# The inverse of a chunked RWKV-7 scan: each level's first product for two heads as one 128-row matmul against zero-padded operands

## The reference, cut to what matters

```python
def step(S, inp):
    r_t, w_t, k_t, v_t, a_t, b_t = inp
    sa = jnp.einsum('bhvk,bhk->bhv', S, a_t)
    S = S * w_t[:, :, None, :] + sa[..., None] * b_t[:, :, None, :] + v_t[..., None] * k_t[:, :, None, :]
    y = jnp.einsum('bhvk,bhk->bhv', S, r_t)
    return S, y
```

## Time and profile before

| | |
|---|---|
| median of three runs | 3730.86 us (3730.16 to 3739.53) |
| span of the profiled execution | 3730.1 us |
| TensorE busy, of the span | 93% |
| VectorE, ScalarE, GpSimd busy | 68%, 40%, 32% |
| the scan: its first matmul of the inverse to its last | 1610.2 to 1941.5 us |
| joint steps in it | 73 |

### The profile page before, as it was taken

One profiled execution on the slowest core, in us unless ns is written; L12 is line 12 of the kernel. 1 busy time (PEld: TensorE's weight loads), 2 busy tenths in 40 slices (PEclk: granted clock), 3 DMA queues, 4 the chain that ended last, 5 costly groups with the idle time before them and its releaser, 6 DMA issues. The chain is left out here.

```text
span 3730.1 us, 55202 instructions
## 1 busy us (share of the span) xinstructions
PE 3484.1 (93%) x23684; PEld 2843.4 (76%) x23684; DVE 2548.5 (68%) x2261; ACT 1510.4 (40%) x1620; POOL 1188.1 (32%) x544
## 2 busy tenths in 40 slices
PE   8999999999999998977788999999998999997996
PEld 6778788887877776667776788887877888886875
DVE  5563767678767875966657667678867888857532
ACT  4563533334443336844446432334454122125322
POOL 1225445445532211243433444555531000000211
PEclk9999999999999999978999999999999999998998
DMA  2112123354312243842323133344312222234422
GB/s 101 39 52 65 55 95 110 102 180 140 115 55 99 79 144 111 261 145 83 105 65 125 48 102 107 103 169 151 106 60 95 84 79 74 79 124 100 146 94 107
DMA packets 218755, 387.50 MB, mean 104 GB/s; under 512 B 16321, under 2 KB 118849, under 8 KB 214529
## 3 DMA queue, kind: packets, MB, share of 16 engines
q1 hardware_dynamic: 180944, 311.62, 26.1%
q10 hardware_dynamic: 37568, 72.36, 5.2%
HBM read 277.50 MB, written 105.91 MB: 103 GB/s over the span
## 5 line engine op out<-in xcount | busy, mean ns | idle before, releaser
L3912 POOL MEMSET ssm_toep<- 128x4096 f32 x1 | 3.5, 3512 | 538.9 <-POOLq L3578 538.9
L3439 DVE SCALAR_TENSOR_TENSOR H<-hy_cu,par,H 128x1024 f32<-128x1024 f32 x120 | 153.5, 1279 | 0.0
L270 POOL TENSOR_TENSOR wlo1C<-fast_raw,whi1C 128x1024 fp32r<-128x1024 f32 (+1 forms) x40 | 112.5, 2813 | 112.7 <-ACT whi1C L260 112.7
L270 POOL TENSOR_TENSOR wlo0B<-fast_raw,whi0B 128x1024 fp32r<-128x1024 f32 (+1 forms) x40 | 113.0, 2825 | 106.0 <-ACT whi0B L260 106.0
L270 POOL TENSOR_TENSOR wlo1A<-fast_raw,whi1A 128x1024 fp32r<-128x1024 f32 (+1 forms) x40 | 111.5, 2787 | 104.0 <-ACT whi1A L260 104.0
L270 POOL TENSOR_TENSOR wlo0A<-fast_raw,whi0A 128x1024 fp32r<-128x1024 f32 (+1 forms) x40 | 110.7, 2768 | 103.5 <-ACT whi0A L260 103.5
L270 POOL TENSOR_TENSOR wlo1B<-fast_raw,whi1B 128x1024 fp32r<-128x1024 f32 (+1 forms) x39 | 107.7, 2762 | 112.1 <-ACT whi1B L260 111.9
L3439 DVE SCALAR_TENSOR_TENSOR hy_odd<-hy_cu,par,hy_odd 128x1024 f32<-128x1024 f32 x112 | 143.3, 1279 | 0.0
L1008 DVE TENSOR_TENSOR fast_xl<-fast_xr,fast_xh 128x2048 fp32r<-128x2048 f32 (+1 forms) x42 | 127.7, 3062 | 21.4 <-ACT fast_xh L849 21.4
L270 POOL TENSOR_TENSOR wlo0C<-fast_raw,whi0C 128x1024 fp32r<-128x1024 f32 (+1 forms) x39 | 108.0, 2768 | 104.1 <-ACT whi0C L260 104.0
L2717 PE MATMUL psA<-sc_XX,sc_NT 64*64 64x32 f32 x2560 | 104.8, 232 | 31.8 <-issue 18.8
(11 more groups left out here) (1459 smaller groups left out, 11601.9 us busy)
## 6 DMA issues: line engine op xcount, KB each, us to landing
fast_raw<-ffn_in_dram SPq DMA_DIRECT2D x88, 512.0 KB, 3.9
fast_xr<-ffn_x SPq DMA_DIRECT2D x28, 1024.0 KB, 6.2
fast_raw<-ffn_out_dram SPq DMA_DIRECT2D x32, 512.0 KB, 3.8
sc_ops<-rw_arbkv SPq DMA_DIRECT2D x14, 1024.0 KB, 6.0
wraw1A<-hybrid_in_dram SPq DMA_DIRECT2D x24, 512.0 KB, 3.5
wraw1B<-hybrid_in_dram SPq DMA_DIRECT2D x24, 512.0 KB, 3.5
ffn_x<-fast_g ACTq DMA_DIRECT2D x22, 512.0 KB, 3.2
ffn_x<-fast_e ACTq DMA_DIRECT2D x22, 512.0 KB, 2.8
```

Source lines behind the costliest of these rows:

```text
L270: eng.tensor_tensor(self.slot(wlo, n), self.raw[n], self.slot(whi, n).bitcast(fp32), ALU.subtract)\
L3439: op = dve.scalar_tensor_tensor(out=acc, in0=c[:, j:j + T], scalar=w, in1=acc, op0=ALU.mult, op1=ALU.add)
L3912: pl.memset(toep[:, :, :], 0.0).then_inc(*tick("st_zero"))
```

## The change

The first product of a tile becomes one matmul for both heads. Its stationary operand is NT of the tile with all 128 rows. Its moving operand is 128 rows x (2 heads x 32 columns) out of a new tensor `XT`, where each head's transposed X stands in the rows of one half and zeros stand in the other half, so that the heads don't mix. The result has 64 partitions, those of `half(m % 2)`, and the heads side by side in the columns. ScalarE brings it to the layout of `Wt` with four copies (two by tile parity and two by head) in place of one. The transposes of VectorE write to `XT`, a ring of three chunks, and wait for the first product of three chunks before; VectorE clears `XT` once at the scan's start. NT's ring goes from six to five, and tensors move in SBUF.

```diff
-                self.XX = at("sc_XX", [P, 4, 2, DT, CHUNK], fp32, 114.5)
-                self.NT = at("sc_NT", [P, 6, DT, CHUNK], fp32, 130.5)
+                self.XX = at("sc_XX", [P, 4, DT, CHUNK], fp32, 113.25)
+                self.XT = at("sc_XT", [P, 3, 2, DT, CHUNK], fp32, 121.25)
+                self.NT = at("sc_NT", [P, 5, DT, CHUNK], fp32, 133.25)
...
-            NTS = 6
+            NTS = 5
+            TURNS = 3
...
+            paired = [b.rearrange("p (e g t) -> p e g t", e=2, g=4) for b in bank]
...
+            def part_of_two(t, l):
+
+                return t.rearrange("p e (g b c) -> p e g b c", b=2, c=2 << l)[:, :, :, 0, :]
...
-                            pe.wait_ge(*after("sc_W", ix + 1))
+                            pe.wait_ge(*after("sc_W", 4 * ix + 4))
...
                         for m in range(DT):
                             if w is not None:
-                                for e in range(2):
-                                    mw = pe.matmul(part_of_tile(eight[iw % 2][half(e), m, :], lw, 0), NT[half(1 - e), iw % NTS, m, :],
-                                                   part_of_tile(XX[half(1 - e), cw % 4, 1, m, :], lw, 0), start=True, stop=True)
+                                mw = pe.matmul(part_of_two(paired[iw % 2][half(m % 2), :, m // 2, :], lw), NT[:, iw % NTS, m, :],
+                                               part_of_two(XT[:, cw % TURNS, :, m, :], lw), start=True, stop=True)
                                 if m == DT - 1:
                                     mw.then_inc(*tick("pe_W"))
...
-                        act.activation(part(Wt[l][:, :, :], l, 0), part(eight[i % 2], l, 0), ACT.Copy).then_inc(*tick("sc_W"))
+                        for q in range(2):
+                            for e in range(2):
+                                act.activation(part_of_two(Wt[l][half(e), q:DT:2, :], l), part_of_two(paired[i % 2][half(q), e, :, :], l),
+                                               ACT.Copy).then_inc(*tick("sc_W"))
...
-                            dve.transpose(XX[half(1 - e), n % 4, 1, :, :].rearrange("p m t -> p (m t)"),
-                                          XX[half(e), n % 4, 0, :, :].rearrange("p m t -> p (m t)")).then_inc(*tick(name))
+                            dve.transpose(XT[half(1 - e), n % TURNS, e, :, :].rearrange("p m t -> p (m t)"),
+                                          XX[half(e), n % 4, :, :].rearrange("p m t -> p (m t)")).then_inc(*tick(name))
...
                     def turned(n):
                         dve.wait_ge(*after("sc_eye_added", n + 1))
+                        if n >= TURNS:
+                            dve.wait_ge(*after("pe_W", order[n - TURNS, LEVELS - 1] + 1))
                         turn_over(n, "sc_turned")
...
                     dve.memset(S[:, 0, :, :], 0.0).then_inc(*tick("sc_S"))
+                    dve.memset(XT[:, :, :, :, :], 0.0).then_inc(*tick("sc_clear"))
+                    dve.wait_ge(*after("sc_clear", 1))
```

More of the change, by code:

```diff
@@ L1441, in __init__ @@
                 self.mask = at("sc_mask", [P, 2, CHUNK], fp32, 96)
[L1442 to L1445, removed]
-                self.XX = at("sc_XX", [P, 4, 2, DT, CHUNK], fp32, 114.5)
-                self.NT = at("sc_NT", [P, 6, DT, CHUNK], fp32, 130.5)
+                self.level = at("sc_level", [P, 5, CHUNK], fp32, 184.75)
+                self.first = at("sc_first", [P, CHUNK], fp32, 96.5)
+                self.eye = at("sc_eye", [P, CHUNK], fp32, 97)
+                self.UV = at("sc_UV", [P, 4, 2, DT, HEAD], fp32, 97.25)
+                self.XX = at("sc_XX", [P, 4, DT, CHUNK], fp32, 113.25)
+                self.XT = at("sc_XT", [P, 3, 2, DT, CHUNK], fp32, 121.25)
+                self.NT = at("sc_NT", [P, 5, DT, CHUNK], fp32, 133.25)
                 self.Wt = [at(f"sc_Wt{l}", [P, DT, CHUNK], fp32, k) for l, k in enumerate((144.25, 146.25, 150.25, 68, 70))]
@@ L2531, in rwkv_scan @@
             RING = 4
-            NTS = 6
+            NTS = 5
+            TURNS = 3
             smask, slevel, sfirst, seye, ops, rt, at = room.mask, room.level, room.first, room.eye, room.ops, room.rt, room.at
-            G, BK, UV, XX, Gx, NT, Wt, Z, S, grown = room.G, room.BK, room.UV, room.XX, room.Gx, room.NT, room.Wt, room.Z, room.S, room.grown
+            G, BK, UV, XX, XT, Gx, NT, Wt, Z, S, grown = (room.G, room.BK, room.UV, room.XX, room.XT, room.Gx, room.NT, room.Wt, room.Z,
+                                                           room.S, room.grown)
             bank = [ps[b // 2][:, b % 2, :] for b in range(8)]
@@ L2723, in inverse @@
                                     mx = pe.matmul(part_of_tile(eight[2 + ix % 2][half(e), m, :], lx, 1), Wt[lx][half(e), m, :],
-                                                   part_of_tile(XX[half(e), cx % 4, 0, m, :], lx, 1), start=True, stop=True)
+                                                   part_of_tile(XX[half(e), cx % 4, m, :], lx, 1), start=True, stop=True)
                                 if m == DT - 1:
@@ L2749, in u_step @@
                             for e in range(2):
-                                mm = pe.matmul(eight[place(("U", n))][half(1 - e), m, :], XX[half(e), n % 4, 0, m, :], Z[half(e), n % 2, m, :],
+                                mm = pe.matmul(eight[place(("U", n))][half(1 - e), m, :], XX[half(e), n % 4, m, :], Z[half(e), n % 2, m, :],
                                                start=True, stop=True)
@@ L2824, in to_xx @@
                         for e in range(2):
-                            act.activation(XX[half(e), n % 4, 0, :, :], G[half(1 - e), n % 4, e, :, 0:CHUNK], ACT.Copy).then_inc(*tick("sc_raw"))
+                            act.activation(XX[half(e), n % 4, :, :], G[half(1 - e), n % 4, e, :, 0:CHUNK], ACT.Copy).then_inc(*tick("sc_raw"))
                     def to_gx(n):
@@ L2902, in begin @@
                     def begin(n):
-                        x = XX[:, n % 4, 0, :, :]
+                        x = XX[:, n % 4, :, :]
                         pl.wait_ge(*after("sc_raw", 4 * n + 2))
@@ L2964, in x_out @@
                             dve.wait_ge(*after("sc_XX", order[n, l - 1] + 1))
-                        mine = part(XX[:, n % 4, 0, :, :], l, 1)
+                        mine = part(XX[:, n % 4, :, :], l, 1)
                         dve.tensor_tensor(mine, part(eight[2 + k % 2], l, 1), mine, ALU.add).then_inc(*tick("sc_XX"))
@@ L3006, in rwkv_scan @@
             passed({f"ring_{b}": sum(incs[b::RING]) for b in range(RING)})
-            passed({n: len(order) for n in ("pe_W", "pe_XX", "sc_W", "sc_NT", "sc_XX")})
+            passed({n: len(order) for n in ("pe_W", "pe_XX", "sc_NT", "sc_XX")})
+            passed({"sc_W": 4 * len(order), "sc_clear": 1})
             passed({n: NC for n in ("sc_first", "sc_eye_added", "pe_Z", "pe_U", "pe_ys", "pe_y", "sc_S")})
```

## The result

| | before | after |
|---|---|---|
| median of four runs each | 3734.8 us | 3960.1 us |
| after to before | | 1.0604 (95%: 1.0582 to 1.0625) |
| span of the profiled execution | 3730.1 us | 3954.5 us |
| inverse, first matmul to last | 331.5 us | 550.2 us |
| granted clock over that stretch | 0.89 | 0.76 |

The kernel is 6.0% slower. Of the 224.4 us by which the spans differ, 218.7 lie in the stretch of the inverse.

The account below looks back on a forecast made before the run. TensorE, the scan's busiest engine, was taken as the bound. 3730 + 281 (pauses with mixed clock) + 2 (ScalarE's copies) + 1 (VectorE's clearing) = 4014 us, range 3850 to 4130.

Parts of the forecast that it names:

- The pause at each change of pattern: Joint steps on TensorE: two pauses a tile, 0.15 us each at full level; a step 3.9 us instead of 0.92.
- TensorE's work becomes the period: Scan: other engines are ready long before, so a period is TensorE's work, 28.5 us at full level, 46 at the lower.
- The share of the lower clock: Scan: two thirds of the time at the lower level, nearer to its first 38 us (78%); +281 us with the pauses.
- the prediction's own formula: Scan period with mixed clock: 28.5 / (1 - 0.67 x (1 - 28.5/46)) = 38.2 us.
- The period before: Scan of the kernel before: a period taken as 18.96 us, so the new one is 19.2 us more, x 14.6.
- ScalarE's copies: Scan: four copies for one, 0.29 us each; up to +9 us in joint steps left to the range, +2 counted altogether.
- Clearing, rings, layout: Scan: VectorE's one clearing counted at +1 us, at most 3; `turned`'s new wait and NT's ring of five at nothing.
- the array's quarters bind: Rival, joint steps: no pause within a step, six records a quarter instead of four; 3733 to 3767 us, chance 0.04.
- the number of records does: Rival, joint steps: 48 records instead of 64 take 0.69 us a step, so faster, 3711 us; chance 0.02.

Follow-up runs that it names:

- group_of_eight: Against the kernel after: a joint step issues its eight wide first products, then its sixteen second products, two pattern changes instead of sixteen; 3716.9 us, ratio 0.9953.
- tall_second: Against the kernel after: second products also take all 128 rows, so no pattern change inside a step, order tile by tile kept; 3718.5 us, ratio 0.9956.
- full_columns: Against the kernel after: the wide first product moves all 128 columns instead of 64, sixteen pauses a step stay; 3956.5 us, ratio 1.0597.

## Why the prediction was right

It gave 4014 us in a range of 3850 to 4130, slower at 0.95; measured are 3960 us.

- **The pause at each change of pattern** held to the hundredth: 0.49 us a tile forecast and measured at the full level, 0.75 and 0.76 at the lower. That two blocks' borders tell what happens sixteen times inside a step was the leap, and group_of_eight and tall_second show it right from two sides. The rule of the Trainium skill, "TensorEngine Tiling (Array Packing)", section Tiling Modes, that changing the mode drains TensorE, agrees with them; it gives no price, and the price here is 0.15 us at one level and 0.22 to 0.25 at the other. The rows show the pause, not what TensorE does in it.
- **TensorE's work becomes the period.** Right: its waits for VectorE's transposes are 5.9 us ahead of the first product instead of 10.2, all at the scan's start, and those for issue are gone. The period at the full level was sized well too. In full_columns two periods at granted clock 1.0 take 32.0 and 34.2 us; their mean, less 5 x 8 tiles x 0.10, is 29 us for the kernel after, against 28.5 forecast:

```profile
1699.44 1.29 DVE L2954 TENSOR_TENSOR sc_G<-psC,sc_mask 128x512 f32<-128x512 f32 x2
...
1731.46 1.29 DVE L2954 TENSOR_TENSOR sc_G<-psD,sc_mask 128x512 f32<-128x512 f32 x2
...
1765.67 1.29 DVE L2954 TENSOR_TENSOR sc_G<-psD,sc_mask 128x512 f32<-128x512 f32 x2
```

- **The share of the lower clock** is the term that I mis-sized most. I took two thirds of the time, from the first 38 us of the kernel before; measured are 48%. With that share the prediction's own formula gives 28.5 / (1 - 0.48 x 0.38) = 34.9 us a period, and the mean of twelve is 35.0. The first 38 us were the wrong neighbour: TensorE stands there for lack of work, up to 1.9 us at once, while inside the new steps it never rests for longer than a pause.
- **The period before** was mis-sized too. The 18.96 us of the earlier trace rows are one period at granted clock 1.0, and the mean is 20.6. That this isn't seen in the sum is luck: with 34.9 us in place of 38.2 it gives 15.9 more a period, x 14.6 = +232 us, and 3965 us in all, 5 us from the result; against 20.6 it gives 14.3 more, +209 us, and 3942, and the 18 us that are then missing I can't place. Of the 54 us by which the forecast was too high, the share of the clock alone is 3.3 x 14.6 = 48.
- **How the +225 divides.** At the full level throughout, a period would be 29 us, 8.4 more than the 20.6 before, which is some 120 us over 14.6 periods; the lower level takes the other 100 or so. That division is worked out, not measured; what full_columns shows is that the clock's part is at least 58.
- **ScalarE's copies** last 0.27 us each (forecast 0.29), but what they cost was under-sized: forecast up to 9 us in the joint steps and left at nothing; 11 us measured with narrow products, where the period is short. In the kernel after TensorE's work covers more of them, and its waits for them are 7.2 and 4.1 us.
- **Clearing, rings, layout:** +1 forecast, 3 measured, at the edge of what can be measured.
- **The rivals.** That the array's quarters bind, and that the number of records does, were given 0.04 and 0.02 and are wrong for this kernel. With the pauses out of the way the time is 3717 us, near the 3711 of the rival in which fewer records gain. That is a near number by another way: the rival had a step of 0.69 us, and the grouped one takes 1.52. What holds of it is that in grouped steps 48 records beat 64, by most of 33 us.

## What to carry to other kernels

Before joining two small matmuls into a tall one, look at the borders between blocks of different rows and columns in the trace of the kernel as it is: where the pattern changes they show a pause that a border of equal patterns doesn't, and an order that alternates pays it every time. If a tall product is worth having for its fewer records, group it: the same instructions went from 6.0% slower to 0.5% faster by their order alone. And of the clock take not a stretch where the engine lacks work as the measure for one where it works with many short pauses.

## What the runs showed of the hardware that I had not expected

- Doubling the columns of 1280 records changed the time by less than 4 us of 3960, because the granted clock rose from 0.76 to 0.94 over the same stretch.
- Eight pauses a step left the granted clock at 0.91 over the inverse, sixteen brought it to 0.76, without any rest of TensorE inside a step longer than a pause.
- TensorE's waits that the profile names "issue", 58 us in the scan before, fell to 23 by grouping 64 matmul records a step and to 6 by grouping 48, although a step got longer by 0.6 us.
